# Two-block layer, split-float32 matmuls: one 512-column pass for the high weights in the MLP and the output projections

## The reference

```python
# first block, MLP
h = jnp.square(jax.nn.relu(u2 @ w_ff1[l]))        # 1024 -> 4096
x = x + gate2 * (h @ w_ff2[l])                    # 4096 -> 1024
...
# second block, output projection, two layers
mix = jnp.concatenate([y_conv.astype(h.dtype), y_ret], axis=-1)     # 2048 features
out = jnp.einsum("bse,ed->bsd", mix, w_out[layer])                  # 2048 -> 1024
x = x + rms_norm(out, post_norm[layer]).astype(x.dtype)
```

## Time and profile before

| | |
|---|---|
| Runs, device time | 949.28, 950.30, 952.63 us; median 950.3 us |
| Profiled execution, span | 949.0 us |
| PE busy / PE weight loads busy | 916.4 us (97%) / 896.8 us (94%) |
| DVE, ACT, POOL busy | 598.6, 498.1, 691.2 us |
| Chain that ended last | PE 86%, DVE 8%, issue 2%, ACT 2%, DMA 1% |

### The profile page before, as it was taken

The page is one execution under the profiler, slowest core; times in us unless marked ns, Lnnn a source line. Parts: engine busy times, 40 slices in busy tenths (PEclk is TensorE's granted clock), DMA queues, the critical chain, the costliest instruction groups (busy, mean ns, idle before and its releaser), DMA issues.

```text
span 949.0 us, 21725 instructions
## 1 busy us (share of the span) xinstructions
PE 916.4 (97%) x7684; PEld 896.8 (94%) x7684; DVE 598.6 (63%) x1122; ACT 498.1 (52%) x820; POOL 691.2 (73%) x898
## 2 busy tenths in 40 slices
PE   5998999999999999999999999999999999999996
PEld 5887999999999999999999999999989999999996
DVE  3889889767776444523566567774366566877522
ACT  3555655575567665555554455445455444544451
POOL 1786587687769877887676758888857667788873
PEclk9999999999999999999999999999999999999998
DMA  9976567654545557554544435655525444455521
GB/s 360 417 300 238 223 225 272 258 185 171 178 175 182 188 211 260 200 190 177 179 155 156 177 133 187 212 183 208 188 89 179 152 158 159 155 213 186 202 86 45
DMA packets 28225, 185.22 MB, mean 195 GB/s; under 512 B 3027, under 2 KB 5504, under 8 KB 6272
## 3 DMA queue, kind: packets, MB, share of 16 engines
q1 hardware_dynamic: 25832, 167.93, 48.9%
q10 hardware_dynamic: 2328, 16.40, 4.8%
HBM read 183.26 MB, written 1.07 MB: 194 GB/s over the span
## 4 chain that ended last, share of the span: by engine, by line
PE 86%; DVE 8%; issue 2%; ACT 2%; DMA 1%; SPq 0%; POOL 0%; ACTq 0%; POOLq 0%; DVEq 0%
PE mm L609 25%; PE mm L611 25%; PE mm L610 25%; PE mm L643 1%; ACT w_hi L1109 1%; DVE ada_raw L1563 1%; DVE w_lo L1525 1%; DVE score L1683 1%; PE ps_o L991 1%; PE ps_s L974 1%; DMA hot<-onehot 1%; PE ps_o L1065 1%; PE mm L627 1%; PE mm L628 1%; PE mm L629 1%
## 5 line engine op out<-in xcount | busy, mean ns | idle before, releaser
L526 POOL TENSOR_TENSOR w_lo<-raw,w_hi 128x256 fp32r<-128x256 f32 x880 | 680.9, 808 | 235.3 <-ACT w_hi L1109 235.2
L609 PE MATMUL mm<-u_hi,w_hi 128*128 128x256 f32 x1568 | 447.2, 285 | 0.5 <-ACT w_hi L1109 0.3
L610 PE MATMUL mm<-u_lo,w_hi 128*128 128x256 f32 x1568 | 435.7, 278 | 0.0
L611 PE MATMUL mm<-u_hi,w_lo 128*128 128x256 f32 x1568 | 435.5, 278 | 0.0
L1109 ACT ACTIVATE w_hi<-raw 128x1024 fp32r<-128x1024 f32 x291 | 307.6, 1058 | 160.0 <-PE mm L611 150.0
L609 PEld LDWEIGHTS mm<-u_hi,w_hi 128*128 128x128 f32 x1568 | 295.7, 189 | 5.8 <-issue 4.9
L610 PEld LDWEIGHTS mm<-u_lo,w_hi 128*128 128x128 f32 x1568 | 295.8, 189 | 2.0 <-issue 1.9
L611 PEld LDWEIGHTS mm<-u_hi,w_lo 128*128 128x128 f32 x1568 | 295.9, 189 | 0.0
L1525 DVE TENSOR_TENSOR w_lo<-raw,w_hi 128x1024 fp32r<-128x1024 f32 x71 | 95.6, 1346 | 64.3 <-ACT w_hi L1109 54.4
L609 PE MATMUL mm<-h_hi,w_hi 128*128 128x256 f32 x256 | 70.8, 277 | 0.0
L610 PE MATMUL mm<-h_lo,w_hi 128*128 128x256 f32 x256 | 70.7, 276 | 0.0
(11 more groups left out here) (350 smaller groups left out, 1323.8 us busy)
## 6 DMA issues: line engine op xcount, KB each, us to landing
raw<-weights SPq DMA_DIRECT2D x145, 1024.0 KB, 4.8
ada_raw<-ada ACTq DMA_DIRECT2D x14, 1024.0 KB, 5.4
ada_raw<-ada SPq DMA_DIRECT2D x6, 1024.0 KB, 9.5
ada_more<-ada SPq DMA_DIRECT2D x4, 1024.0 KB, 12.1
bias<-tab_scratch SPq DMA_DIRECT2D x1, 1536.0 KB, 9.4
dec<-decay ACTq DMA_DIRECT2D x1, 1536.0 KB, 7.0
x<-xT SPq DMA_DIRECT2D x1, 1024.0 KB, 10.7
out<-x SPq DMA_DIRECT2D x4, 256.0 KB, 2.3
```

The lines of the kernel that those rows point to most:

```text
L526: ins = nc.gpsimd.tensor_tensor(lo[:, at], r[:, at], hi[:, at], ALU.subtract)
L609: nc.tensor.matmul(dst, wh, rhs_hi(k), start=a, stop=False)
L610: nc.tensor.matmul(dst, wh, rhs_lo(k), start=False, stop=False)
L611: i = nc.tensor.matmul(dst, wl, rhs_hi(k), start=False, stop=b)
```

## The change

1. `u_hi` and `u_lo` become the two halves of one tile `u_both`, and likewise `h_both` and `mix_both`, so that both can be one moving operand of 2 x 256 columns.
2. A new `pair_unit` issues two matmuls for each block: high weights on both halves, 512 columns into the whole bank, then low weights on the high half, 256 columns added into the first half of the bank. The second half of the bank holds lo·hi and must be added.
3. It is used in 27 units of F1 (all behind the first five), in 24 of F2 (not in the fourth output block of either turn of the loop) and in 14 of out in each layer (not in the last output block). Each has 8 blocks: 79 units, 632 blocks. The other units stay as they were.
4. F1: ACT copies the second half into `z_part`; DVE adds it to the first half into `z_full`, then squares relu in one instruction from `z_full` twice into `h_full`; ACT copies that into `h_hi` instead of squaring `relu_h`; DVE subtracts as before.
5. F2: DVE adds the second half to `x` in an instruction of its own. Out: ACT copies the second half (`o_part`), DVE adds (`o_sum`), and ACT's square and scaling read `o_sum`.

```diff
+        def pair_unit(g, c, o, both, ready=None, first=True, last=True, turn=(8, 2)):
+            w_hi_, w_lo_ = rounded(g, c)
...
+            for k in range(KC):
...
+                at = slice(k * P, (k + 1) * P)
+                a, b = (first and k == 0), (last and k == KC - 1)
+                nc.tensor.matmul(mm[o % 4][:, 0:2 * T], w_hi_[:, at], both(k), start=a, stop=False)
+                i = nc.tensor.matmul(mm[o % 4][:, 0:T], w_lo_[:, at], both(k)[:, 0, :], start=False, stop=b)
+            i.then_inc(S["unit_done"], 1)
```

ACT in F1:

```diff
+                    A(z_part[:, f % 2, :], mm[o % 4][:, T:2 * T], ACT.Copy).then_inc(S["z_part"], 1)
+                    if f >= 6:
+                        high(g, c + SLOTS)
+                    act.wait_ge(S["hf_ready"], lin(g, 8, f - EARLY + 1))
...
-                    A(relu_h[:, f % 2, :], mm[o % 4][:, 0:T], ACT.Relu).then_inc(S["relu_made"], 1)
...
+                    A(dst, h_full[:, f % 2, :], ACT.Copy).then_inc(S["hh_ready"], 1)
```

DVE in F1:

```diff
-                if f >= 6:
-                    dve.wait_ge(S["unit_done"], lin(g, 8, c + 1))
-                    low(g, c - 1 + SLOTS)
-                dve.wait_ge(S["relu_made"], lin(g, 8, f + 1))
...
+                    dve.wait_ge(S["z_part"], f - EARLY + 1)
+                    V.tensor_tensor(z_full[:, f % 2, :], mm[o % 4][:, 0:T], z_part[:, f % 2, :], ALU.add)\
+                        .then_inc(taken[o % 4], 1)
+                    dve.wait_ge(taken[o % 4], o // 4 + 1)
+                    V.scalar_tensor_tensor(h_full[:, f % 2, :], z_full[:, f % 2, :], 0.0, z_full[:, f % 2, :],
+                                           ALU.max, ALU.mult).then_inc(S["hf_ready"], 1)
+                    dve.wait_ge(S["hf_ready"], f - EARLY + 1)
+                    if f >= 6:
+                        low(g, c - 1 + SLOTS)
```

DVE behind F2:

```diff
+                    if j % 4 < 3:
+                        own(V.scalar_tensor_tensor(x[:, j, :], mm[o % 4][:, T:2 * T], mod[:, GATE2, j:j + 1], x[:, j, :],
+                                                   ALU.mult, ALU.add))
```

ACT behind out:

```diff
+                if q == 1 and j < KC - 1:
+                    A(o_part[:, j % 2, :], mm[o % 4][:, T:2 * T], ACT.Copy).then_inc(S["o_part"], 1)
+                    high(None, c + SLOTS)
+                    act.wait_ge(S["o_summed"], (KC - 1) * l + j + 1)
+                    square_x(3 + 2 * l, j, o_sum[:, j % 2, :])
+                    A(o_out[:, j, :], o_sum[:, j % 2, :], ACT.Identity, scale=col("post", KC * l + j))\
+                        .then_inc(taken[o % 4], 1)
```

DVE behind out:

```diff
+                if q == 1 and j < KC - 1:
+                    dve.wait_ge(S["o_part"], (KC - 1) * l + j + 1)
...
+                    V.tensor_tensor(o_sum[:, j % 2, :], mm[(oA + 64 + j) % 4][:, 0:T], o_part[:, j % 2, :], ALU.add)\
+                        .then_inc(S["o_summed"], 1)
```

More of the change, by code:

```diff
@@ L145, in _build @@
     keep("step_u", [P, 8])
-    u_hi = keep("u_hi", [P, KC, T], F32R)
-    u_lo = keep("u_lo", [P, KC, T], F32R)
+    u_both = keep("u_both", [P, 2, KC, T], F32R)
+    u_hi, u_lo = u_both[:, 0, :, :], u_both[:, 1, :, :]
     keep("step_raw", [P, 8])
@@ L287, in _build @@
         part_turn = tile_in(early, "part_turn", [P, 2, T])
-    mix_hi = p3("mix_hi", [P, 2 * KC, T], F32R)
-    mix_lo = p3("mix_lo", [P, 2 * KC, T], F32R)
+    mix_both = p3("mix_both", [P, 2, 2 * KC, T], F32R)
+    mix_hi, mix_lo = mix_both[:, 0, :, :], mix_both[:, 1, :, :]
     ret = p3("ret", [P, RH, T])
@@ L308, in _build @@
     o_out = p3("o_out", [P, KC, T])
+    o_part = cc
+    o_sum = th_c
     rows = p3("rows", [P, 3, T])
@@ L612, in unit @@
                 i.then_inc(S["unit_done"] if q == parts - 1 else S["part_done"], 1)
+        def pair_unit(g, c, o, both, ready=None, first=True, last=True, turn=(8, 2)):
+            w_hi_, w_lo_ = rounded(g, c)
+            per_c, per_o = turn
+            pe.wait_ge(S["hi_ready"], lin(g, per_c, c + 1))
+            low_ready(g, c, per_c)
+            if first and o >= 4:
+                pe.wait_ge(taken[o % 4], lin(g, per_o, o // 4))
+            for k in range(KC):
+                if ready is not None:
+                    ready(k, k)
+                at = slice(k * P, (k + 1) * P)
[3 more added lines that the diff above has]
+            i.then_inc(S["unit_done"], 1)
         def first_units(n, c, o, ready, hi=u_hi, lo=u_lo, warm=None, behind=None, w=T):
@@ L942, in _ @@
                         pe.wait_ge(S["hl_ready"], KC * (q + 1))
-                    unit(g, U_F2 + 4 * j + q, O_F2 + j, lambda k: h_hi[:, q * KC + k, :],
-                         lambda k: h_lo[:, q * KC + k, :], first=q == 0, last=q == 3, turn=(16, 1))
+                    if j < 3:
+                        pair_unit(g, U_F2 + 4 * j + q, O_F2 + j, lambda k: h_both[:, :, q * KC + k, :],
+                                  first=q == 0, last=q == 3, turn=(16, 1))
+                    else:
+                        unit(g, U_F2 + 4 * j + q, O_F2 + j, lambda k: h_hi[:, q * KC + k, :],
+                             lambda k: h_lo[:, q * KC + k, :], first=q == 0, last=q == 3, turn=(16, 1))
                     if j == 0 and q == 0:
@@ L1088, in _ @@
                     rd = (lambda s: lambda k, t: pe.wait_ge(S[s], KC * l + k + 1))("mixr_ready" if q == 0 else "mixc_ready")
+                if j < KC - 1:
+                    pair_unit(None, uA + 64 + n, oA + 64 + j, (lambda off: lambda k: mix_both[:, :, off + k, :])(off),
+                              ready=rd, first=q == 0, last=q == 1)
+                    continue
                 unit(None, uA + 64 + n, oA + 64 + j,
```

39 lines of the change are left out of this document (21 added, 18 removed).

## The result

The changed kernel takes **960.2 us** (median of 5 runs, 958.90 to 961.29) against 950.4 for the kernel before, run beside it (median of 5, 949.28 to 952.63): a ratio of 1.0094, with a 95% interval of 1.0064 to 1.0123. It is 9.8 us slower. The forecast was 944.0 us and faster; the time lies above its range, and on the other side of no change.

A forecast was written before the change was run, and what follows sets the result against it. PE's matmul stream was taken as the bound, with weight loads pacing 256-column matmuls at 0.1133 us. Gains of F1 1.5 + F2 2.2 + out 2.6 = 6.3 us took 950.3 to 944.0 us, range 941.5 to 949.3.

The forecast's parts named there:

- 0.215 us: PE, changed blocks: the 512-column split matmul streams in 0.215 us, twice 256 columns, hiding the low weights' load of 0.11.
- the gain of 7.3 us: PE, all 79 changed units: blocks of 0.328 us against 0.340 save 0.093 us a unit, if PE never waits.
- the slower rival: All 79 units: 512 columns from two SBUF places stream at float32 rate, 0.43 us; 632 blocks cost 128 us, 1078; 5%.
- 512 at half of 0.43: PE: float32 passes take 0.43 us for 512 columns, in proportion to columns; split columns were put at half.
- The second term: PE, changed blocks: the 256-column matmul behind the long one keeps 0.1133 us, paced by loading the next high weights.
- upper bound of 0.336 us: PE, changed block: 0.218 + 0.118 us if the slower pace behind long streams holds; gain 2.5 us in all.
- A fixed cost per matmul: Rival, PE: 0.1133 us is 0.107 of stream plus 0.006 fixed, so only 3.8 us is saved, about 947.3; 25%.
- F1 bound by ACT and DVE: Rival, F1: rounds average 2.9 us over PE's 2.63; F1 gains nothing or loses up to 4.9, 945.5 to 950.4; 14%.
- a load that is hidden entirely: Rival, PE: block of 0.322 us, gain 11.4 us less 1.2 for F1's start, 940.1; 9%.
- F1's start: F1, unit 10: `w_hi` starts 0.7 to 1.1 us later and POOL follows; counted as 0.7 to 1.2 us lost.
- The new square on DVE: F1: reading two SBUF operands into PSUM, it takes 0.4 to 0.9 us, as a sign of being right.
- A 512-column distance over 0.22 us: PE: sign that the forecast is wrong, against 0.215 us from a 512-column matmul's start to the next if right.

The follow-up runs named there:

- width sweep: Changed kernel, halves contiguous, with one high-weight matmul per block of out's changed units, 64 to 512 columns wide, low-weight product left out: 954.4 us in one run.
- single long matmul: Changed kernel with blocks again three 256-column matmuls, except one 512-column matmul in each turn of F2 and one in first-layer out: 955.6 us, ratio 1.0037.
- cut statistics: Kernel before, with its eight 512-column float32 statistics each written as two of 256 columns: 951.4 us against 951.7, ratio 1.0006.
- first experiment: Changed kernel with all added copies and additions, but three 256-column matmuls in each block: 951.4 us against 952.4 for the kernel before, ratio 0.9979.

## Why the prediction was wrong

**The step that failed** is the term "I take **0.215 us** as an estimate for 512 split columns". It measured 0.226 us at best, as the first behind an even stretch, and 0.235 in the kernel. At 0.226 the block is 0.226 + 0.1133 = 0.339 us and the gain of 7.3 us is as good as nothing; at 0.235 it is a loss. The slip stands in the sentence before the term: a distance of 0.1133 was taken to bound the stream of 256 columns at "at most half of a float32 pass's 0.215". Half of 0.215 is 0.1075, and 0.1133 allows more than that. I had concluded from the floor (one column as slow as 128) that the load sets the pace of 256 columns, and taken that for leave to think the stream shorter. The floor is real and the width sweep shows it, but a floor of 0.112 under a distance of 0.1133 says only that the load takes no longer than the matmul; it does not say that the stream is shorter than the load. The trace of before could not tell the two apart at 256 columns, and the sum should have run from 0.215 to at least 2 x 0.1133 = 0.227, the stream as long as its distance. I had that number: it stands in the prediction as the point from which the slower rival decides, but there it was tied to a float32 stream of 0.43 us and given 5%.

**The analogy that carried it:** "512 at half of 0.43". Float32 passes keep to twice columns / 2.4 (0.43 for 512), and split streams above the corner do not keep to columns / 2.4. The Trainium skill (TensorE: Matmul & The Clock Gate, section Back-to-back issue gap) gives N/2.4 + 2.5 ns for the isolated gap of one matmul, by estimate 215.8 for 512, which is close to the term; the runs here show 226 to 236. The Trainium skill's other form there, N/1.2 at the lower clock, agrees with the sweep above its floor to the nanosecond (220 for 264 columns, 400 for 480). The 131 ns that the same section of the Trainium skill gives for a sustained stream of 512 columns is seen in no run here.

**The second term:** the 256-column matmul behind the long one, taken as 0.1133 and measured at 0.118. The upper bound of 0.336 us for the block named the right rhythm from the right rows (behind 512-column passes, 0.117), and I set it aside because "0.117 stands in the trace where stages have just changed or float32 work is mixed in". The single long matmul and, in the trace, the cut statistics show that the long passes themselves bring it on. With 0.118 and a stream of 0.235 the sum comes out: 632 x 0.0133 = 8.4 us slower.

**Rivals.** The slower rival decided from a distance of 0.227 us, and the measured 0.235 is beyond that; the test was right, its mechanism was wrong. It blamed the two places in SBUF, which cost nothing, and its price of 0.203 us a block was 15 times too high. A fixed cost per matmul would have left a gain of 3 us; there is none. F1 bound by ACT and DVE is not seen, nor is a load that is hidden entirely at a block of 0.322 us.

**What held.** Most of what was said of the other engines. The added copies and additions cost nothing that the time shows (first experiment). F1's start was delayed, somewhat less than reckoned; the rows of the changed kernel beside the earlier trace rows, ACT and then POOL:

```profile
295.65 1.07 ACT L1140 ACTIVATE w_hi<-raw 128x1024 fp32r<-128x1024 f32 x1
...
296.96 3.71 POOL L530 TENSOR_TENSOR w_lo<-raw,w_hi 128x256 fp32r<-128x256 f32 x5 [2.77 <-ACT w_hi L1140]
```

`w_hi` of unit 10 starts 0.77 us later than before (0.7 to 1.1 was said), and POOL behind it 0.79 us later. That it falls into the range is luck in part: ACT itself comes to unit 5 0.23 us later in this execution (293.53 against 293.30), and from there to that `w_hi` it takes 2.12 us, 0.54 more than before, where 2.3 to 2.7 was said. PE lost only some 0.2 us by it and not 0.7, since it was itself behind: unit 10 starts at 300.07, not at 299.0. The new square on DVE took what the earlier trace rows had promised (ns min/median/max; 0.4 to 0.9 us was said, and the longest is a little over it):

```profile
L1978 DVE SCALAR_TENSOR_TENSOR ps_t<-z_full x27: 432/674/984, 294.6 to 363.5; 128x256 f32<-128x256 f32 x27
```

The end is unchanged, 13.49 us from the second layer's last matmul of out in both kernels; behind the first layer's out it is not quite (`diag`, 0.38 us). "A 512-column distance over 0.22 us" was named as what would make the forecast wrong, and it was.

## What to carry to other kernels

Before you merge matmuls to save weight loads, find out whether the load or the stream sets their pace: a floor that shorter matmuls also show does not tell, only a wider one does. Here the floor that goes with the load of 128x128 weights is as long as the stream of 256 columns, so at 256 columns or more the load is hidden and a merge saves instructions but no time. And give a term that decides the sign its own worst case: "twice what the trace shows for half" was 0.227 us, and it was enough to turn the forecast.

## What I had not expected of the hardware

**Two rhythms at one clock.** At a granted clock of 1.00 throughout, the same 256-column matmul has a distance of 0.113 us or of 0.118. One 512-column pass among them, split or float32, changes 0.113 into 0.118 for 16 us and more. In the kernel before it ends where short float32 passes or a wait come in between; with the long ones in groups of eight it ended as soon as 256s followed each other (in the sweep it did so behind one such group and not behind another, where a wait lay between). Why the effect of one long pass can last longer than that of eight is open; so is the cause of the rhythms.

**A surcharge that grows with the stream, at the higher clock only:** about 7 ns over columns / 2.4 at 256 columns, 13 at 288, 17 at 480, and none over columns / 1.2 at the lower level. Nothing here shows where it comes from.

**The floor follows the clock too:** it is 0.112 us at the higher level and 0.213 at the lower, so the corner stays at about 256 columns.

**A version that beats both kernels** was not found. The kernel before still has 1703 distances of 0.116 to 0.120 us, some 7.5 us over 0.113; cutting its long passes removed some 400 of them, two thirds of that gain went into a wait, and the rest can't be told from the scatter of the runs. What starts the others was not tried.
